# An encoder step on one core: x is transposed unscaled while w_ada loads, and the bias rows are written later, from DRAM to DRAM

## What is computed

```
sh1, sc1, g1, sh2, sc2, g2 = split(silu(c) @ w_ada + b_ada)        # per sequence, 9 sequences
h = rmsnorm(x, norm1_g) * (1 + sc1) + sh1
za, zg, q, k, v = split(h @ w_in)
y_conv = silu(layernorm(causal_dwconv([left, za * sigmoid(zg)], w_dw) + b_dw))
o = band attention(q, k, v) with a relative-position bias per head
x = x + g1 * (concat(y_conv, o) @ w_out)
x = x + g2 * peer(rmsnorm(x, norm2_g) * (1 + sc2) + sh2)           # top-16 of 128*128 experts, 8 heads
y = rmsnorm(x, final_g)
```

## Time and profile before

| | |
|---|---|
| median of 3 runs | 4136.48 us (4126.74 to 4151.48) |
| the profiled execution | 4124.8 us, of it 4123.0 us span |
| TensorE busy | 3596.5 us, 87% |
| VectorE busy | 2763.0 us, 67% |
| ScalarE, GpSimd busy | 470.0 us and 1122.0 us |
| HBM traffic | 1401.82 MB, mean 340 GB/s |
| mean granted TensorE clock | 0.937 |

### The profile page before, as it was taken

One profiled execution on the slowest core, in us unless ns is written; L12 is line 12 of the kernel. 1 busy time (PEld: TensorE's weight loads), 2 busy tenths in 40 slices (PEclk: granted clock), 3 DMA queues, 4 the chain that ended last, 5 costly groups with the idle time before them and its releaser, 6 DMA issues.

```text
span 4123.0 us, 33620 instructions
## 1 busy us (share of the span) xinstructions
PE 3596.5 (87%) x11871; PEld 1896.9 (46%) x11871; DVE 2763.0 (67%) x4972; ACT 470.0 (11%) x1125; POOL 1122.0 (27%) x858
## 2 busy tenths in 40 slices
PE   4699998987988789689689999999868999996992
PEld 0366644456553564355634444444353444442441
DVE  2128872227888886679877666676797766655677
ACT  1100002210000350011800000000080000000000
POOL 1100000005453543345043222222404322222233
PEclk8899999999999689889999999999989999998996
DMA  9978753349999999899199999999919999999997
GB/s 351 233 229 259 245 197 124 117 146 382 400 400 416 390 369 362 326 373 385 67 410 421 421 419 408 421 421 419 401 67 391 419 421 420 420 420 390 422 413 308
DMA packets 356524, 1401.82 MB, mean 340 GB/s; under 512 B 22352, under 2 KB 146456, under 8 KB 219109
## 3 DMA queue, kind: packets, MB, share of 16 engines
q0 software_dynamic: 116720, 831.77, 50.5%
q1 hardware_dynamic: 239072, 563.91, 36.8%
q10 hardware_dynamic: 576, 4.19, 0.2%
HBM read 1369.87 MB, written 31.42 MB: 340 GB/s over the span
## 4 chain that ended last, share of the span: by engine, by line
DMA 47%; PE 27%; issue 11%; DVE 10%; POOL 3%; ACT 1%; another core or an unknown queue 0%; SPq 0%; DVEq 0%; POOLq 0%; ACTq 0%
DMA R<-in_u_experts,MS 33%; PE bank L805 10%; DMA R<-in_v_experts,MS 8%; PE bank L781 8%; PE bank L985 4%; DVE R L1819 3%; POOL R L677 3%; DMA R<-in_w_ada 2%; DVE R L2021 2%; PE bank L735 1%; DMA R<-in_w_out 1%; DVE R L1818 1%; PE bank L712 1%; DVE R L1909 1%; DMA R<-in_w_pq 1%
## 5 line engine op out<-in xcount | busy, mean ns | idle before, releaser
L677 POOL DMA_INDIRECT R<-in_u_experts,MS x640 | 921.5, 1440 | 1757.1 <-DVE MS L1909 1496.8
L1909 DVE CUSTOM_DVE_ANT_0 R<-R 128x2048 f32<-128x2048 f32 x368 | 845.0, 2296 | 413.6 <-DMA R<-in_u_experts,MS 401.3
L1151 PE MATMUL bank<-R,RB 128*128 128x512 f32 x2304 | 1020.6, 601 | 78.6 <-DMA R<-in_v_experts 78.6
L1151 PE MATMUL bank<-RB 128*128 128x512 f32 x1792 | 778.2, 592 | 0.0
L1151 PEld LDWEIGHTS bank<-R,RB 128*128 128x128 f32 x2304 | 441.9, 193 | 647.2 <-issue 553.0
L1909 DVE CUSTOM_DVE_ANT_0 R<-R,RB 128x2048 f32<-128x2048 f32 x272 | 622.5, 2289 | 117.8 <-DMA R<-in_u_experts,MS 116.8
L805 PE MATMUL bank<-R,RB 128*128 128x512 f32 x1216 | 532.0, 599 | 22.7 <-DMA R<-in_w_out 11.8
L1151 PEld LDWEIGHTS bank<-RB 128*128 128x128 f32 x1792 | 340.5, 190 | 428.5 <-issue 428.5
L781 PE MATMUL bank<-RB,R 128*128 128x256 f32 (+1 forms) x1536 | 401.7, 423 | 28.4 <-DMA R<-in_w_pq 22.1
L2021 DVE SCALAR_TENSOR_TENSOR R<-R,MS 128x2048 f32<-128x2048 f32 x128 | 301.4, 2355 | 183.0 <-DMA R<-in_v_experts,MS 181.7
L805 PEld LDWEIGHTS bank<-R,RB 128*128 128x128 f32 x1216 | 232.6, 192 | 316.8 <-issue 289.8
(11 more groups left out here) (296 smaller groups left out, 2033.4 us busy)
## 6 DMA issues: line engine op xcount, KB each, us to landing
R<-in_v_experts SPq DMA_DIRECT2D x144, 1024.0 KB, 9.1
RB<-in_v_experts SPq DMA_DIRECT2D x112, 1024.0 KB, 9.1
R<-in_w_ada SPq DMA_DIRECT2D x48, 2048.0 KB, 12.9
R<-in_w_in SPq DMA_DIRECT2D x32, 2048.0 KB, 18.3
R<-in_w_out SPq DMA_DIRECT2D x16, 2048.0 KB, 11.6
R<-in_w_pq SPq DMA_DIRECT2D x16, 2048.0 KB, 18.0
R<-in_u_experts,MS POOLq DMA_INDIRECT x640, 11.5
RB<-in_x_prompt POOLq DMA_DIRECT2D x6, 1024.0 KB, 15.2
```

The lines of the kernel that those rows point to most:

```text
L677: pool.indirect_dma_start(dst, None, table, bass.IndirectOffsetOnAxis(ap=expert[T_ % 2][:, c:c + 1], axis=0)).then_inc(signal, 16)
L1151: x = pe.matmul(PB[4 * h + q][:, :], W[:, i, h * P:(h + 1) * P], vring[slot][:, q * PW:(q + 1) * PW], start=(i == 0), stop=(i == NKEY - 1))
L1909: V.tensor_tensor_reduce(u, u, x, 1.0, 0.0, ALU.mult, ALU.add, dots[t % 2][:, h * TOPK + s:h * TOPK + s + 1]).then_inc(dots_done, 1)
```

## The change

x is transposed unscaled after the 6th and the 7th block of w_ada, and `mrow` block by block, two blocks late. Only PSUM banks 0 to 2 hold x, bank 3 holds the transposed `mrow`. ACT copies every group, those of the sample rows too. The cached convolution rows are transposed before the last two pieces of w_ada. When `A1T` is there, `hTX` is scaled in place by ACT and `hTY` in place by DVE, block by block, and the first unit waits for each block by itself (`scaled`). `mrow` moves to partitions 32 to 40, as `hTX` is now written while it is in use. The loop of the units is written out once for its first pass.

For the bias rows, one row of each head is stored early; its 127 copies are made from DRAM to DRAM after the modulation rows have been saved; `biasN` and `biasC_d` are filled after the attention of the first two tiles.

```
-        mrow = rb(0, 2 * D, NCND)
+        mrow = RB[32:32 + NCND, CX:CX + 2 * D]
-            sp.wait_ge(s_ext, 16)
+            sp.wait_ge(s_ext, 32)
             sp.wait_ge(s_conv, 1)
...
             pool.wait_ge(s_setE, 2)
-            pool.wait_ge(mod_done, NM1)
-            dma(ext_d[:, :, :], ext.unsqueeze(1).to_broadcast([NH, P, EXT])).then_inc(s_ext, 16)
-            pool.wait_ge(s_ext, 16)
-            for b in range(NB):
-                dma(biasN[NS * b:NS * b + NS], bass.AP(tensor=ext_d, offset=511,
-                    ap=[[EXT - 1, NS], [P * EXT, NH], [1, NS]])).then_inc(s_bn, 16)
-            for h in range(NH):
-                dma(biasC_d[h].rearrange("(b s) n -> b s n", s=NS),
-                    rows(ext_d, [[0, NB], [EXT - 1, NS]], P, h * P * EXT + 383)).then_inc(s_bc, 16)
+            dma(ext_d[:, 0, :], ext).then_inc(s_ext, 16)
             pool.wait_ge(mod_free, 4 + NM)
             dma(mod_d[:, 2 * D:], mrow2).then_inc(mod_saved, 16)
+            pool.wait_ge(s_ext, 16)
+            dma(ext_d[:, 1:, :], ext_d[:, 0:1, :].to_broadcast([NH, P - 1, EXT])).then_inc(s_ext, 16)
...
             pool.wait_ge(pv_done, NH)
             for t in range(TX):
                 dma(x1[t], xp[t]).then_inc(s_x5x, 16)
+            pool.wait_ge(s_ext, 32)
+            for b in range(NB):
+                dma(biasN[NS * b:NS * b + NS], bass.AP(tensor=ext_d, offset=511,
+                    ap=[[EXT - 1, NS], [P * EXT, NH], [1, NS]])).then_inc(s_bn, 16)
+            for h in range(NH):
+                dma(biasC_d[h].rearrange("(b s) n -> b s n", s=NS),
+                    rows(ext_d, [[0, NB], [EXT - 1, NS]], P, h * P * EXT + 383)).then_inc(s_bc, 16)
...
+            def turn_mods(m):
+                pe.wait_ge(mod_free, 4 + 2 * (m + 1))
+                for k in range(4 * m, 4 * m + 4):
+                    t = pe.transpose(PB[3][:, 16 * k:16 * k + 9], mrow[:, k * P:(k + 1) * P], ident[32:32 + NCND, 32:32 + NCND])
+                t.then_inc(s_modT, 1)
+            def turn_x(g0, g1):
+                pe.wait_ge(s_xn, T)
+                for g in range(g0, g1):
+                    if g >= 3:
+                        pe.wait_ge(xT_act, g - 2)
+                    for i in range(4):
+                        src = xt[i][:, g * P:(g + 1) * P] if g < KT else xt[TP][:, (4 * (g - KT) + i) * P:][:, 0:P]
+                        t = tr(PB[g % 3][:, i * P:(i + 1) * P], src, P)
+                    t.then_inc(xT_done, 1)
+            def turn_conv_cache():
+                pe.wait_ge(s_cc, 32)
+                pe.wait_ge(xT_act, KT + 4)
+                for c2 in range(4):
+                    if c2 == 3:
+                        pe.wait_ge(cc_E, 1)
+                    for i in range(4):
+                        c, h = 2 * c2 + i // 2, i % 2
+                        t = tr(PB[c2 % 3][:, i * 120:(i + 1) * 120], ccx[:, h, c * P:(c + 1) * P], 120)
+                    t.then_inc(cc_T, 1)
...
                 mm.then_inc(mod_done, 1)
-            pe.wait_ge(mod_free, 4 + NM1)
-            for k in range(2 * KT):
-                t = tr(PB[4][:, 16 * k:16 * k + 9], mrow[:, k * P:(k + 1) * P], NCND)
-            t.then_inc(s_modT, 1)
-
-            pe.wait_ge(s_xn, T)
-            for g in range(KT + 4):
...
+                if half and m >= 2:
+                    turn_mods(m - 2)
+                if half and m == 5:
+                    turn_x(0, 10)
+                if half and m == 6:
+                    turn_x(10, KT + 4)
+                    turn_conv_cache()
+            turn_mods(6)
+            turn_mods(7)
...
                 for k in range(KT):
+                    if scaled:
+                        pe.wait_ge(xT_act, KT + 4 + k + 1)
+                        pe.wait_ge(xT_dve, k + 1)
...
+            act.wait_ge(s_setE, 6)
+            for g in range(KT + 4):
+                act.wait_ge(xT_done, g + 1)
+                if g < KT:
+                    A(hTX[:, g], PB[g % 3][:, 0:NX], ACT.Copy)
+                    A(hTY[:, g, 0:NPY], PB[g % 3][:, NX:NP], ACT.Copy).then_inc(xT_act, 1)
+                else:
+                    A(hTY[:, 4 * (g - KT):4 * (g - KT) + 4, NPY:NY], PB[g % 3][:, :].rearrange("p (k n) -> p k n", k=4),
+                      ACT.Copy).then_inc(xT_act, 1)
             act.wait_ge(s_A1, 1)
+            act.wait_ge(xT_act, KT + 4)
             for k in range(KT):
-                act.wait_ge(xT_done, k + 1)
-                A(hTX[:, k], PB[k % 4][:, 0:NX], ACT.Identity, scale=A1T[:, k, 0:1], bias=modT[:, k, 0:1])
-                A(hTY[:, k, 0:NPY], PB[k % 4][:, NX:NP], ACT.Identity, scale=A1T[:, k, 0:1],
-                  bias=modT[:, k, 0:1]).then_inc(xT_act, 1)
+                A(hTX[:, k], hTX[:, k], ACT.Identity, scale=A1T[:, k, 0:1], bias=modT[:, k, 0:1]).then_inc(xT_act, 1)
             act.sem_inc(z_free, 2)
...
-            for m in range(4, 8):
+            for m in range(4, 7):
                 first_block(m)
+            for c2 in range(4):
+                dve.wait_ge(cc_T, c2 + 1)
+                CP(uS[:, 2 * c2:2 * c2 + 2, :, 0:CTX].rearrange("p c b k -> p (c b) k"),
+                   PB[c2 % 3][:, 0:480].rearrange("p (a k) -> p a k", k=CTX)).then_inc(cc_E, 1)
+            V.memset(uP[:, :, 0:CTX], 0.0)
+            first_block(7)
+            dve.wait_ge(s_modT, 8)
...
+            dve.wait_ge(xT_act, KT + 4)
+            for k in range(KT):
+                o = hTY[:, k, NPY:NY].rearrange("p (b s) -> p b s", s=NS)
+                ch.mark(TT(o, o, A1T[:, k, 1:9].unsqueeze(2).to_broadcast([P, NB, NS]), ALU.mult))
+                TS(hTY[:, k, 0:NPY], hTY[:, k, 0:NPY], A1T[:, k, 0:1], modT[:, k, 0:1], ALU.mult, ALU.add)
                 ch.sync()
+                TT(o, o, modT[:, k, 1:9].unsqueeze(2).to_broadcast([P, NB, NS]), ALU.add).then_inc(xT_dve, 1)
```

More of the change, by code:

```diff
@@ L748, in _, with project @@
                 mm.then_inc(mod_done, 1)
-            pe.wait_ge(mod_free, 4 + NM1)
-            for k in range(2 * KT):
-                t = tr(PB[4][:, 16 * k:16 * k + 9], mrow[:, k * P:(k + 1) * P], NCND)
-            t.then_inc(s_modT, 1)
-            pe.wait_ge(s_xn, T)
-            for g in range(KT + 4):
[L756 to L776, removed]
+                if half and m >= 2:
[7 more added lines that the diff above has]
+            turn_mods(7)
+            def project(srcs, weights, par, signal, scaled=False):
                 for k in range(KT):
+                    if scaled:
+                        pe.wait_ge(xT_act, KT + 4 + k + 1)
+                        pe.wait_ge(xT_dve, k + 1)
                     w = weights[:, k]
@@ L785, in _, with glu_and_modulation @@
             pe.wait_ge(cc_E, 4)
-            with pe.Fori(0, 4) as i:
+            def glu_and_modulation(i, first):
                 for b in range(2):
@@ L790, in _ @@
                         pe.wait_ge(z_free, i * 4 + (2 * b + c + 1))
-                        project((hTX, hTY), ring[:, b, :, c * P:(c + 1) * P], c, z_done)
+                        project((hTX, hTY), ring[:, b, :, c * P:(c + 1) * P], c, z_done, first and b == c == 0)
                         for a in range(2 * c, 2 * c + 2):
@@ L794, in _ @@
                             modulate(i * 8 + (NM1 + 4 * b + a), a, 2 + a % 2)
+            glu_and_modulation(0, True)
+            with pe.Fori(1, 4) as i:
+                glu_and_modulation(i, False)
             loaded = [8, 8, 20, 20]
@@ L1177, in _ @@
             A(rs, tmpa, ACT.Sqrt).then_inc(s_r1, 1)
+            act.wait_ge(s_setE, 6)
[7 more added lines that the diff above has]
+                      ACT.Copy).then_inc(xT_act, 1)
             act.wait_ge(s_A1, 1)
-            act.wait_ge(s_setE, 6)
+            act.wait_ge(xT_act, KT + 4)
             for k in range(KT):
-                act.wait_ge(xT_done, k + 1)
-                A(hTX[:, k], PB[k % 4][:, 0:NX], ACT.Identity, scale=A1T[:, k, 0:1], bias=modT[:, k, 0:1])
-                A(hTY[:, k, 0:NPY], PB[k % 4][:, NX:NP], ACT.Identity, scale=A1T[:, k, 0:1],
-                  bias=modT[:, k, 0:1]).then_inc(xT_act, 1)
+                A(hTX[:, k], hTX[:, k], ACT.Identity, scale=A1T[:, k, 0:1], bias=modT[:, k, 0:1]).then_inc(xT_act, 1)
             act.sem_inc(z_free, 2)
@@ L1545, in _ @@
                 TS(xt[t], xt[t], rs[:, t:t + 1], None, ALU.mult).then_inc(s_xn, 1)
-            for m in range(4, 8):
+            for m in range(4, 7):
                 first_block(m)
-            dve.wait_ge(s_modT, 1)
-            ch.link(CP(modT[:, :, 0:9], PB[4][:, :].rearrange("p (k c) -> p k c", c=16)[:, :, 0:9]))
+            for c2 in range(4):
[5 more added lines that the diff above has]
+            dve.wait_ge(s_modT, 8)
+            ch.link(CP(modT[:, :, 0:9], PB[3][:, :].rearrange("p (k c) -> p k c", c=16)[:, :, 0:9]))
             STT(out=A1T[:, :, 0:9], in0=modT[:, KT:, 0:9], scalar=1.0,
@@ L1552, in _ @@
             dve.wait_ge(s_A1, 1)
[L1554 to L1560, removed]
-                ch.sync()
[L1562 to L1572, removed]
```

(4 more changed lines are left out.)

## The result

| | before | after |
|---|---|---|
| median | 4131.61 us (4122.50 to 4151.48, 4 runs) | 4083.31 us (4079.18 to 4086.87, 4 runs) |
| profiled execution | 4124.8 us, span 4123.0 | 4083.83 us, span 4082.0 |

The ratio is 0.987, with a 95% interval of 0.9844 to 0.9896: faster, by 43 to 64 us of 4131.6. The two profiled executions differ by 41 us. The median lies inside the range and the direction is the forecast's. The size is not: the sum gave 32.6 us on the trace, and the trace shows 43.2 us at the second unit. The likeliest case assumed a wait that does not hold. That the median lies in the range is owed to its lower end, which was set by rival A less the spread of runs, and not to the sum.

The account below looks back on a forecast made before the run. Transfers (47%) and TensorE (27%) were taken to bound it, with two holes at the start: 13.7 + 19.9 = 33.6 us, less 1, gives 32.6. So 4124.8 becomes 4092.2, on the median 4104 us; range 4081 to 4125.

Parts of the forecast that it names:

- rival A: First unit: increment of `z_free` passes queued activations, unit starts one block after the scales, 6.5 us earlier, 4097 us; chance 0.10.
- The two holes: TensorE gaps before the first unit (122.1 to 152.9 us) and the second (173.4 to 196.9); gains 13.7 and 19.9 us.
- Work put between the pieces: Transposes inserted between the last w_ada pieces of the start: last piece ends at 126.1 instead of 122.1 us, costing 4.0 us.
- rival D: Start: TensorE works at half clock through the inserted transposes; gain 21 us, 4115 us; chance 0.11.
- The lower bound of 122.5 us: End of the start's last w_ada piece if all the inserted work runs at the full clock.
- To the scales: From the last w_ada piece to `A1T`: DVE's sums, 8 narrow transposes, `modT` and `A1T`; 126.1 to 131.7 us.
- Scaling in place: First unit waits for all 16 ACT scales, 7.3 us, and begins at 139.2 us, 13.7 us earlier than at 152.9.
- The transfer gone: Between first two units: without `ext` queued, two w_ada pieces take 3.6 us; second unit at 163.3 us against 196.9.
- The late copy and the bias reads: 127-fold copy at 503 us takes 18 to 30 us, costs nothing; 24 read issues take 13.9 us on POOL.
- The 1 us charged: Cost (0 to 4 us) for late bias reads meeting a w_out load and for the code written out once more.
- B: Late copy starves the weights as the old write did: 18 us idle, net 15, 4122 us; chance 0.12.
- C: Late copy runs on few DMA engines, delaying ACT's squares 115 us: net 82 us slower, 4219 us; chance 0.05.

Follow-up runs that it names:

- e4: Kernel before with only the bias rows' part of the change (copy from DRAM to DRAM, late reads), x as before; 4110.03 us, ratio to before 0.9949.
- e5: Changed kernel with the bias rows written 128-fold from 16 SBUF partitions at about 174 us, beside the third unit; 4128.27 us.
- e1_hold: Changed kernel with ScalarE waiting for the end of its 16 scales before it frees the first unit's two PSUM banks; 4087.54 us.
- e2: Changed kernel with ScalarE freeing the first unit's two PSUM banks before its first scale; 4079.74 us.
- after_again: The changed kernel measured once more, unaltered; 4082.28 us, ratio to before 0.9887.
- e8: Changed kernel with PSUM banks freed before the scales and 32 unused identity transposes while TensorE waits ahead of the first unit; 4080.48 us, ratio to before 0.9873.
- e3: Changed kernel with the bias rows' old place and form put back, so only the change in x remains; 4127.59 us, ratio to before 0.9984.
- e6: Changed kernel with the 127-fold DRAM to DRAM copy issued at the old write's place, about 123 us; 4090.15 us.

## Why the prediction was off in size, step by step

**What bounds it: right.** The two holes, the queue behind the second, the 102 GB/s and 18 GB/s, and that the shift reaches the experts whole: all seen. e4 and e5 confirm the reading of the queue.

**Work put between the pieces: forecast 4.0 us, measured 0.8.** The last piece ends at 122.9, not 126.1 us; and piece 12, ahead of all that was inserted, had itself ended 0.7 us later than before (101.5 against 100.7), so the insertion cost next to nothing. One part is a misreading of the loop: `turn_mods` does 4 transposes a block, not 8 (0.5 us, not 1.1). The larger is the price of a group of x: 40 transposes took 5.4 us, 0.545 us a group instead of 0.65, and the cached rows 2.0 us, not 2.6. 0.65 had been taken for a clock of 0.84; it was 0.95 from 101 to 108 us and 1.00 from 108 to 123, and what was left is ScalarE's pace, 20 copies in 5.3 us, 0.53 us a group. The transposes themselves end the idle time between the pieces, and the pieces behind them run at 1.8 us each. So rival D, half the clock through the transposes, did not happen. Its ground was misread too: between 90 and 100 us both pieces of the kernel before took 3.6 us, at a granted clock of 0.50, not every other one, and even so the clock came back once the transposes filled the gaps. The lower bound of 122.5 us does not come out of its terms either: they give 123.3 us with 0.55 us a group, 121.5 with 0.46.

**To the scales: forecast 5.6 us, measured 4.5** (122.9 to 127.4), with the 4 transposes instead of 8 in it.

**Scaling in place: this is the step that failed.** "The unit also waits for `z_free`, and ACT's `act.sem_inc(z_free, 2)` still stands behind all its 16 scales", priced at 7.5 us with the hand-over. The wait is there, but the increment does not wait for the activations in front of it to end: 2.3 us, not 7.5. e1_hold shows what the forecast described (8.2 us, at 0.50 us a scale and not 0.455), e2 how much the place of the increment costs (1.3 us). Rival A, at 0.10, had the mechanism in so many words, and I argued it away with "an engine takes its instructions in order". It does, but taking is not ending. A put the unit one block behind the first scale, at 1.0 us; that is e2's start, and the changed kernel's lies 1.3 us behind it. The Trainium skill has a line that I did not weigh: "Advanced Engine Details and Errata" (Engine Queue Depths) gives ScalarE a depth of 8. An estimate by it: the increment would come when 8 scales are left, about 4 us in. It came after 2.3, with 11 or 12 not yet ended. The trace agrees that ScalarE takes instructions ahead, and does not bear out 8 as the limit of what the increment can pass.

**The transfer gone: right.** Forecast 20.5 + 3.6 us from the first unit to the second, measured 20.4 + 3.6. The 20.4 is one draw, as much of it is clock: the same unit took 19.3 us in after_again and 17.5 in e8. e3 adds what the text did not say: it listed 13.7 us from the first hole as if they could be had without the second part. Alone they are worth 0.7 us.

**The late copy and the bias reads: right on cost, high on the charge.** The copy landed after 30.0 us, at the upper end of 18 to 30, and the v stores behind it after 29.9; no engine waited for either. 24 issues took 14.0 us of POOL against 13.9. The 1 us charged was not seen: 43.2 us at the second unit are 43.2 us at the first gather. By the Trainium skill, "DMA: Bandwidth & Descriptors" (Latency and other measured facts), the estimate was 25 us, for another row pitch; the measured 30.0 us include the modulation save ahead and the weights beside it, so that no run here tests the page's figure. Rivals B and C did not happen: during the copy POOL's queue moved 6.5 MB in 35 us.

**The sum.** 3.2 + 1.1 + 5.2 us of late starts that did not come, and 1.0 us of charge: 10.5 us. 32.6 + 10.5 = 43.1, measured 43.2. The medians differ by 48.3 us, 5 more than the trace explains, and those of e3 and e4 show the same surplus. The runs of before spread over 29 us, those of after over 8 and, taken again, over 25; and the experts' stage alone lies between 3184.4 us (e6) and 3204.3 us (e3_x_only) in the ten profiles. The time goes with the mean granted clock: of the 13 runs of before beside e1 to e4, the four slowest (4146 to 4154 us) are the four at 0.926 to 0.930, the others (4126 to 4137 us) lie at 0.933 to 0.940. I put the 5 us down to that spread; no experiment shows it, and the cause stays open.

## What to carry to other kernels

- A semaphore increment that an engine issues by itself, behind queued work, did not say here that the work had ended. Find out which one a wait needs before pricing it: attach the increment to the last instruction where the data matter, and put it ahead of the queue where only a buffer does.
- When two holes lie one behind the other, ask what sets the end of the second. If it is a transfer with its own start, shortening the first is worth nothing until the transfer goes, and then both are gained at once: 0.7 and 19.6 us alone, 43.2 together.
- The write from 16 SBUF partitions cost more than its bytes, wherever it stood. Judge a transfer by what the other queue still gets while it runs.
- The time of one run can't place a change of 13 us in this kernel (e6: 13 us in the trace, 6 in the time). The place in the trace can.

## What was unexpected of the hardware

- ScalarE's increment took effect when about 4 of the 16 activations in front of it had ended (its waiter began 2.3 us after the first of them, at 0.5 us each, in all five profiles with that order).
- The same 5.2 MB in the same place made TensorE wait 39.9 us when they came from 16 SBUF partitions (e3) and 11.2 us when they came from DRAM (e6).
- While the write from SBUF ran, both DMA queues got as many packets (785 and 786), and the weights 20 GB/s.
- Some 6 us with hardly any work ahead of the first unit cost 3.0 us of clock: the granted clock stood at its lower level (1.2 GHz) from 126 to 135 us. 32 transposes of no use in that gap kept it at the upper one.
